# GpSimd's rounding of each weight unit in two instructions of 512 columns instead of one of 1024

## What is computed

```
# first block
h = rmsnorm(x, attn_norm)
z = h @ w_in                       # pooled branch, q, k, v, gates
a = pool_mixer(u_pool, w_pool, pool_scale)
b = swa_sink_attention(q, k, v, sinks)
x = x + (g_pool * a + g_attn * b) @ w_out
h = rmsnorm(x, ffn_norm)
up = causal_depthwise_conv(h @ w_up, conv_w, conv_b)
x = x + (silu(gate) * val) @ w_down
# second block, 16 meta tokens in front
proj = rms_norm(h) @ w_in_2
o_dn = gated_deltanet_group(...)   # both directions, chunks
o_at = axial_gqa_group(...)        # full attention with axial rope
h = h + rms_norm(concat(o_dn, o_at) @ w_out_2)
f = square(relu(rms_norm(h) @ w_up_2)) @ w_down_2
h = h + rms_norm(f)
```

## Time and profile before

| | |
|---|---|
| median of three runs | 1442.71 us (1441.52 to 1447.87) |
| the profiled execution | 1444.77 us, its span 1441.0 us |
| mean granted TensorE clock in the span | 0.985 |
| busy: TensorE / VectorE / ScalarE / GpSimd | 1369.1 / 700.1 / 433.4 / 895.4 us |
| loads of `raw` | 204, 512 KB each, 3.4 us to landing |

### The profile page before, as it was taken

The page is one execution under the profiler, slowest core; times in us unless marked ns, Lnnn a source line. Parts: engine busy times, 40 slices in busy tenths (PEclk is TensorE's granted clock), DMA queues, the critical chain, the costliest instruction groups (busy, mean ns, idle before and its releaser), DMA issues.

```text
span 1441.0 us, 20446 instructions
## 1 busy us (share of the span) xinstructions
PE 1369.1 (95%) x7304; PEld 1110.5 (77%) x7304; DVE 700.1 (49%) x1119; ACT 433.4 (30%) x842; POOL 895.4 (62%) x1042
## 2 busy tenths in 40 slices
PE   7999999899999999999899999899989999999996
PEld 5877777678888887887778886648767888888885
DVE  7788767744444445113667874595552111211113
ACT  3344444422121222112354444434522111111111
POOL 6856644367777777775656653414266767777772
PEclk9999999999999999999999999999999999999998
DMA  5322211133232332322121111000022332322321
GB/s 196 108 83 70 92 59 59 44 103 114 93 102 89 100 97 92 101 88 88 59 73 45 60 45 59 15 1 3 19 98 73 102 102 87 102 93 97 102 87 58
DMA packets 31883, 113.84 MB, mean 79 GB/s; under 512 B 3536, under 2 KB 3920, under 8 KB 31696
## 3 DMA queue, kind: packets, MB, share of 16 engines
q1 hardware_dynamic: 31680, 112.85, 23.8%
q10 hardware_dynamic: 144, 0.18, 0.0%
HBM read 110.92 MB, written 2.10 MB: 78 GB/s over the span
## 4 chain that ended last, share of the span: by engine, by line
PE 88%; DVE 5%; ACT 4%; issue 2%; DMA 0%; SPq 0%; DVEq 0%; ACTq 0%
PE ps L1068 43%; PE ps L1282 19%; PE ps L1419 7%; ACT arena L578 3%; PE ps L1087 2%; PE ps L1101 2%; PE ps L1302 2%; PE ps L1393 1%; PE ps L1122 1%; PE ps L1223 1%; PE ps L1374 1%; PE ps L1185 1%; PE ps L1523 1%; PE ps L1524 1%; PE ps L1661 1%
## 5 line engine op out<-in xcount | busy, mean ns | idle before, releaser
L491 POOL TENSOR_TENSOR w_lo<-raw,w_hi 128x256 fp32r<-128x256 f32 (+1 forms) x804 | 646.8, 834 | 40.9 <-ACT w_hi L578 25.0
L483 POOL TENSOR_SCALAR w_hi<-raw 128x1024 fp32r<-128x1024 f32 (+1 forms) x188 | 200.9, 1069 | 405.4 <-issue 359.9
L1068 PE MATMUL ps<-h_hi,w_hi 128*128 128x512 f32 x928 | 369.0, 398 | 2.3 <-DVE arena L2397 2.2
L1068 PE MATMUL ps<-h_lo,w_hi 128*128 128x512 f32 x928 | 362.2, 390 | 0.0
L1068 PE MATMUL ps<-h_hi,w_lo 128*128 128x512 f32 x928 | 362.0, 390 | 0.0
L1068 PEld LDWEIGHTS ps<-h_hi,w_hi 128*128 128x128 f32 x928 | 174.6, 188 | 47.7 <-issue 10.3
L1068 PEld LDWEIGHTS ps<-h_lo,w_hi 128*128 128x128 f32 x928 | 174.7, 188 | 38.5 <-issue 2.8
L1068 PEld LDWEIGHTS ps<-h_hi,w_lo 128*128 128x128 f32 x928 | 174.7, 188 | 36.9
L578 ACT ACTIVATE arena<-ps 128x512 f32<-128x512 f32 (+6 forms) x199 | 95.0, 510 | 233.0 <-PE ps L1122 58.7
L578 ACT ACTIVATE arena<-arena 128x512 f32<-128x512 f32 (+6 forms) x192 | 102.0, 535 | 203.6 <-DVE arena L2397 134.3
L1282 PE MATMUL ps<-g_hi,w_hi 128*128 128x512 f32 x400 | 155.7, 389 | 0.9 <-DVE arena L2008 0.9
(11 more groups left out here) (284 smaller groups left out, 1822.0 us busy)
## 6 DMA issues: line engine op xcount, KB each, us to landing
raw<-in_w_stream SPq DMA_DIRECT2D x204, 512.0 KB, 3.4
out<-xT SPq DMA_DIRECT2D x8, 256.0 KB, 2.1
xT<-in_x_t SPq DMA_DIRECT2D x1, 1056.0 KB, 8.3
xT<-in_x_t SPq DMA_DIRECT2D x1, 792.0 KB, 6.1
C<-in_cst SPq DMA_DIRECT2D x1, 576.0 KB, 9.8
arena<-in_cst SPq DMA_DIRECT2D x1, 528.0 KB, 4.4
xT<-in_x_t SPq DMA_DIRECT2D x1, 264.0 KB, 3.9
arena<-in_pos SPq DMA_DIRECT2D x1, 256.0 KB, 4.1
```

The source lines that it names most:

```text
L483: pool.tensor_scalar(w_hi[j][:, k0:KT, :], raw[j % 2][:, k0:KT, :], 1.0, 1.0, ALU.mult, ALU.mult).then_inc(S["pool_step"], 1)
L491: low = pool.tensor_tensor(w_lo[j][:, k:k + n, :], raw[j % 2][:, k:k + n, :], w_hi[j][:, k:k + n, :], ALU.subtract)
L1068: last = mm(dst[p], w[:, k, :], h[:, k, cols], start=(k == 0 and n == 0), stop=(k == KT - 1 and n == 2))
```

## The change

In rounds from 1 on in which GpSimd rounds, the rounding is done in two instructions of four tiles (512 columns) each, in order; the semaphore is raised by the second. Round 0 is left as it was.

```diff
--- before.py
+++ after.py
@@ -480,7 +480,10 @@
                         if isinstance(i, int) and i == 0 and j == 0:
                             k0 = 4
                             pool.tensor_scalar(w_hi[0][:, 0:4, :], raw[0][:, 0:4, :], 1.0, 1.0, ALU.mult, ALU.mult).then_inc(S["w_first"], 1)
-                        pool.tensor_scalar(w_hi[j][:, k0:KT, :], raw[j % 2][:, k0:KT, :], 1.0, 1.0, ALU.mult, ALU.mult).then_inc(S["pool_step"], 1)
+                        n = KT if isinstance(i, int) and i == 0 else KT // 2
+                        for k in range(k0, KT, n):
+                            high = pool.tensor_scalar(w_hi[j][:, k:min(k + n, KT), :], raw[j % 2][:, k:min(k + n, KT), :], 1.0, 1.0, ALU.mult, ALU.mult)
+                        high.then_inc(S["pool_step"], 1)
                         if isinstance(i, int) and i == 0:
                             pool.wait_ge(S["w_first"], 1)
                             pool.wait_ge(S["pool_step"], j + 1)
```

## The result

The changed kernel takes 1447.44 us (median of 17 runs, 1445.44 to 1449.42), the kernel before in the same sessions 1443.53 us (17 runs, 1441.28 to 1447.87). The ratio is 1.0019, with a 95% interval of 1.0011 to 1.0028: slower by 2.7 us, 1.6 to 4.0; the two medians lie 3.9 us apart, inside that. The runs scatter by several microseconds and the profiles are one execution each, so what follows compares single stretches of the traces, and takes the size of an effect from the ratios.

The account below looks back on a forecast made before the run. TensorE, busy 1369.1 of 1441.0 us, was taken as the bound. Steady stages 0, VectorE chains -0.2 and the place ahead of the last up-projection +1.0 gave +0.8 us on 1442.71: 1443.5 us, range 1439.5 to 1447.5.

Parts of the forecast that it names:

- the forecast's own bounds: Whole kernel: -1.3 to +1.7 us around the median before, plus 2 us of clock each side, giving 1439.5 to 1446.5.
- rival (b): Ahead of the last up-projection: each half takes 852 ns, eight units take 5.2 us more, 1447.5 us in all; chance 0.15.
- Cost on GpSimd: GpSimd, 184 units: two halves at 612 ns against 1.05 us, 0.17 us more per unit, 31 us of busy time.
- Hidden in the steady stages: Long stage of 1008 matmuls: GpSimd idles 1.48 us per unit, so the extra 0.17 us fits; priced at nothing.
- a sign of being wrong: Steady stages: a wait of TensorE for GpSimd turning up there would show the forecast wrong.
- VectorE's chains: VectorE behind roundings at L1913, L2074 and L2085: shorter turns gain 0.2 us in all, ends 0 and 1.3.
- The three operations: L1913, L2074 and L2085 on VectorE, each ending with a rounding: forecast to end 0.39, 0.49 and 0.46 us earlier.
- Rival (a): VectorE's three hits give 1.3 us, the reserve holds, 1.5 us less slow clock: 1440 us; chance 0.25.
- The reserve: Eight units ahead of the last up-projection: 1.4 us more work against GpSimd's 1.36 us to spare; +1.0 us, ends 0 and 1.7.
- VectorE's part: VectorE's chain of five ahead of the last up-projection: first and fifth operations meet later subtractions, 0.37 us each, 0.7 more.
- The clock: TensorE's slow stretches at 1.2 GHz behind waits: a shifted gap may catch more or less, 2 us allowed on both sides.

## Why the prediction was right, and what it missed

It forecast +0.8 us, and 1439.5 to 1447.5. The ratio gives +2.7 us, 1.6 to 4.0, so even the lower end is twice the forecast. The median of 1447.44 lies 0.06 us inside the range, and above 1446.5, where the forecast's own bounds end: the last microsecond was put there for rival (b), which is out. So the direction and the place were right, and that the time fell inside the range is luck. Point by point:

*Cost on GpSimd.* 0.17 us per unit were forecast from the row of 612 ns, 31 us in all. Two halves take 1.21 us, 0.16 more, and the total rose by 33.9. Rival (b), 852 ns, is out.

*Hidden in the steady stages.* Right in the long stage: 1.32 us of idle time are left, and with 176 units in halves the ratio is 0.9999. But the forecast named only one place of small reserve, and there is another at the start of round 5: the wait of 0.60 us at 121 us, near to what it had given as a sign of being wrong. VectorE's wait behind it took that up.

*VectorE's chains.* I took a gain of 0.2 us, and the result is about 0. The three operations came forward nearly as worked out, L2088 by more, because it ran ahead of the first half and met none; those behind them paid part of it back. But the path to TensorE was wrong. I had read that VectorE works without a break up to the 3.12 us for L2139; in fact it stood 1.24 us for ScalarE just ahead of that, and its gain of 0.73 us went into that wait, which rose by 0.63. Rival (a) is out, and for this reason, not because the blocks stayed long. The Trainium skill, "SBUF — State Buffer", section "Who interferes with whom", says that the later of two such instructions is blocked for the whole of the other one. The trace agrees on the single block, which halved, 0.91 to 0.47 us; what the rule doesn't speak of is whether TensorE waits for the blocked engine, and that decided.

*The reserve.* This is the step that carries the result. I took 1.0 us, TensorE's idle time rose by 1.11, with GpSimd as the releaser. The parts differ: GpSimd came 2.1 us later measured from the last sum, where I had worked out 2.7, and its reserve was smaller than 1.36, because 0.34 us pass from its last split to the first matmul (1073.54 to 1073.88). VectorE's part was 0.25 in the run with the wait where the unit is used (0.33 in the changed kernel's own trace: 5.20 us for the chain of five, 4.87 before) and not 0.7 to 1.1: its fifth operation was stretched by 0.47 us, but the first met nothing more (0.78 for 0.81) and the second lost less than before (0.98 for 1.09).

*The clock.* This is the term of the sum that was mis-sized. I allowed 2 us of slow clock on both sides as scatter, and put nothing into the sum. In this pair of profiles TensorE ran at 1.2 GHz for longer behind the longer wait: 44 matmuls in 12 us before, 40 after, and 0.9 us more for the group. With 1.11 it makes 2.0 of the 2.7 us. The remaining 0.7 lies within the interval of the ratio, and I have no row for it.

That the slow stretch belongs to the longer wait, and not to where it happened to fall, isn't shown. For it speak the two kernels with halves in the eight units (24.80 and 24.63 us for the group, behind 7.54 and 7.41) against the two with whole ones (23.91 and 23.41, behind 6.43 and 6.44). Against it: 24.13 us behind 12.14 with quarters, 24.92 behind only 6.68 with the wait where the unit is used, and with a group of three 17.97 us for 72 matmuls behind 6.73 where it was 18.48 behind 6.43. And behind the second wait of 2.24 us the 1.6 us of slow stretch comes in some profiles and not in others. How often it comes with either kernel would decide over the rest, and single profiles can't say. So of the 2.7 us the wait of 1.11 is shown, and the other 1.6 stay open.

## What to carry to other kernels

Judge a cost on a side engine by its smallest reserve, not by its mean: GpSimd was idle a quarter of the steady stage, and the loss came from the one stretch in which it worked through eight units without a gap and TensorE waited for the eighth. Cutting an instruction in two to let another engine in between pays only where somebody waits for that engine: here VectorE came free 0.73 us earlier at one place and then stood waiting for ScalarE, while the added fixed part was paid in full where GpSimd was the last. So follow the freed engine to its next wait before counting the gain. And where a group waits for all of its members first, ask whether it may start on three: a group of three, with the sum of squares in the middle of the fourth unit, gained 3.5 us on the kernel before, more than the change had cost.

## What I had not expected of the hardware

A cut-up instruction can cost far more beside a busy VectorE than its fixed part. Four quarters took 1.50 us alone and 3.24 us beside VectorE's chain; two halves took 1.21 alone and 1.97 beside it, one whole rounding 1.05 and 1.38. The pieces aren't all alike in this: a whole rounding took 1.99 us at 119.87 us in the kernel before. The numbers fit each piece waiting for a turn of its own; no run separates that from another cause.

Two buffers for the raw weights were just enough for GpSimd's pace of 4.3 us per unit. When ScalarE took the roundings over, waits for the load came forward at once, up to 5.20 us.

VectorE's busy time rose by 8.6 us with the change, of which L2022, a subtraction of two operands in the down-projections, took 5.8 (from 862 to 970 ns each, 54 times), all of it beside TensorE's matmuls; TensorE's list of waits has none for it:

```profile
L2022 DVE TENSOR_TENSOR g_lo<-arena,g_hi 128x512 fp32r<-128x512 f32 x54 | 51.9, 970 | 206.1 <-ACT g_hi L581 206.1
```
